# Token lists read ahead of the third expert's weights, kept lists on ScalarE's queue, a short tile's entries on 128 partitions, the eighth expert's weights early

## The chip, the core and the metric

The kernel runs on one NeuronCore of a Trainium2 chip. The metric is device time in microseconds of one execution; the figure for a kernel is the median of several runs. The engines are TensorE (PE), VectorE (DVE), ScalarE (ACT), GpSimd (POOL) and SyncE (SP), which only issues transfers. All transfers run on the core's 16 DMA engines.

## What is computed

One layer of a hybrid decoder: sparse attention with an indexer, a causal pooling branch, a gated merge, a layer norm, a mixture of 64 routed experts (8 per token) with one shared expert, and a second norm with a gated embedding. It works on 512 prompt tokens and 64 sample tokens, 576 rows of width 1024, in float32. The part that matters here:

```python
def moe(h, w_router, router_bias, w_exp13, w_exp2, w_sh13, w_sh2):
    s = jax.nn.sigmoid((h @ w_router).astype(jnp.float32))
    sb = s + router_bias.astype(jnp.float32)
    ...                                     # best 4 of 8 groups, then 8 of 64 experts: eidx
    gate = jnp.take_along_axis(s, eidx, axis=1)
    gate = gate / jnp.sum(gate, axis=-1, keepdims=True) * ROUTED_SCALE
    ...
    y = swiglu(h, w_sh13, w_sh2)            # shared expert
    for e in range(N_EXPERTS):
        y = y + combine[:, e:e + 1] * swiglu(h, w_exp13[e], w_exp2[e])
    return y
```

## The kernel before

The program is written by hand for each engine: every engine has its own list of instructions, runs it strictly in order, and waits on semaphores. PSUM banks go round: a list of jobs made by `plan_banks` gives every product its bank, and the order of each engine must follow that list. The 576 rows are five tiles, four of 128 rows and a last one of 64 (`ROWS`).

The stage of the change lies between the first norm and the expert loop. For every tile TensorE turns the normed rows, computes the router's scores and, later, the shared expert's up product (`shared_up`, job `s13`). VectorE's `route` picks 8 experts per row (mask `selM`), TensorE's `rank` counts with triangular products how many rows before chose the same expert, `pick_gates` puts the gates into `rec`, and `list_goals` turns the rank into a place in a token list and signals `goal_ready`. GpSimd's `enter` then writes the rows' entries (row number, choice number, gate) to the lists in DRAM, one indirect transfer for each of the 8 choices of a tile: forty in all, eight for the tile of 64 rows as well. Each of the 64 experts has one list.

When all entries are in, the lists come back to SBUF as `listed`: for three experts of each four the first 96 entries ("main"), for every fourth expert, whose weights are kept over three passes, 32 entries for each pass ("kept"). SyncE reads them in six transfers (lines 796 and 797). ScalarE repeats the row numbers (`spread`), TensorE turns them (lines 1638 to 1640, job `lists`), VectorE makes row numbers and gates of them (2153 to 2156) and signals `index_ready`; only then GpSimd can gather rows (983).

The expert loop has 48 passes. A pass has 128 rows, 96 of three quarters of a main expert's rows and 32 of the kept expert: the up product (line 1659, 64 matmuls of 32 columns each), the activation, the down product (1672), and an indirect write of the results. GpSimd gathers two passes ahead, in four pieces; VectorE turns the gathered rows (`turn_x`, 2135). The weights of an expert are 3 MB, 2 up and 1 down; there are five slots: three for main experts, two for kept ones (0 and 4). SyncE issues their loads in one fixed order (`load_main`, `load_kept`; up half line 759, down half 762), each behind a wait for the pass that frees the slot: up halves for `up`, down halves for `down`.

Around the change the shared expert's second part runs on TensorE: it turns the gated products (job `s13T`, line 1295, read out by ScalarE at 1047) and multiplies them by `w_sh2` (job `s2`, lines 1631 and 1308), two halves for each tile; VectorE adds them to the rows (2147). In that series stand the turning of the lists, after the second tile, and VectorE's first `turn_x`, after the fourth. The loop's first product waits until all `s2` halves are read. `w_sh13` and `w_sh2` lie in two ring slots at `RING`; slot 4 of the experts lies over both, so expert 7 (the eighth, kept) is loaded when the last `s2` half is done. The order of SyncE there is written out:

```python
            sp.wait_ge(goal_ready, NT)
            filled(sp, ("s13T", NT - 1))
            load_main(2)
            sp.wait_ge(entered, 16 * NT * TOPE)
            ...                                   # six list reads
            filled(sp, ("s2", NT - 1, 1))
            load_kept(1)
```

Of the kernel before, what the change touches and what calls it, by code (L numbers as in the profile page):

```python
# [95 lines left out]
def constants():  # L96
# [22 lines left out]
    rec[:, :, :, 1] = rec[:, :, :, 0] * TOPE + np.arange(TOPE)[None, None, :]  # L119
    put("rec", rec)  # L120
# [31 lines left out]
SMALL_HEADS = 2 * H  # L152


def plan_banks():
# [100 lines left out]
    for t in range(NT):  # L256
        for c in range(2) if t < 4 else (1,):
            add(("s2", t, c), "dve")
        if t == 1:
            add(("lists",), "dve")  # L260
# [3 lines left out]
def build(nc, a, o):  # L264
# [14 lines left out]
    with ctx:  # L279
# [153 lines left out]
        SLOTS = [LG + WSLOT * s for s in range(4)] + [RING]  # L433
        w13 = [at(where, KT * 512).rearrange("p (k n) -> p k n", k=KT) for where in SLOTS]
        w2 = [at(where + 16 * KB, 2 * D).rearrange("p (k n) -> p k n", k=2) for where in SLOTS]

# [5 lines left out]

        def list_row(n):
            return n % 3 * (PASSES // 3) + n // 3
# [13 lines left out]
        yt = [at(where, HALF * D).rearrange("p (j n) -> p j n", j=HALF) for where in (RING, LG + 40 * KB, LG + 56 * KB)]  # L458
        wpin = at(LG, 2 * D).rearrange("p (k n) -> p k n", k=2)
        g2, b2 = at(RING + 24 * KB, D), at(RING + 28 * KB, D)  # L460
# [16 lines left out]
        lists = nc.dram_tensor("token_lists", [NE * LIST, 4], F32, kind="Internal").ap()  # L477

# [87 lines left out]
        listed_in = sem("lists_in")  # L566
# [138 lines left out]
        def _(sp):  # L705
# [81 lines left out]
            sp.wait_ge(goal_ready, NT)  # L787
            filled(sp, ("s13T", NT - 1))
            load_main(2)


            sp.wait_ge(entered, 16 * NT * TOPE)
            by_four = lists.rearrange("(q j n) k -> j q n k", j=4, n=LIST)
            per = PASSES // 3
            for i in range(3):
                sp.dma_start(listed[per * i:per * i + per, 0:CAP, :], by_four[i][:, 0:CAP, :]).then_inc(listed_in, 16)
                sp.dma_start(listed[per * i:per * i + per, CAP:P, :], by_four[3][:, 32 * i:32 * i + 32, :]).then_inc(listed_in, 16)
            extra = further_blocks(sp)
            filled(sp, ("s2", NT - 1, 1))
            load_kept(1)  # L800
# [45 lines left out]
        def _(pool):  # L846
# [198 lines left out]
        def _(act):  # L1045
# [181 lines left out]
            for t in range(1, NT):  # L1227
                shared(t)
# [6 lines left out]
            act.wait_ge(listed_in, 96)  # L1235
            copy(spread, listed[:, :, 0].rearrange("p (g i) -> p g i", g=4).unsqueeze(2).broadcast_to([PASSES, 4, 4, 32])).then_inc(spread_ready, 1)
# [51 lines left out]
        def _(pe):  # L1288
# [329 lines left out]
            for t in range(NT):  # L1618
                pe.wait_ge(sha_ready, t + 1)
                turn4(("s13T", t), [shact[t][0:ROWS[t], P * k:P * k + P] for k in range(2)], ROWS[t])  # L1620
            w = weights(pe, "sh2")
            for t in range(NT):
                read(pe, ("s13T", t))
# [9 lines left out]
                if t == 1:  # L1633
                    pe.wait_ge(listed_in, 96)
                    pe.wait_ge(spread_ready, 1)
                    b = claim(pe, ("lists",))
                    for g in range(4):
                        nc.tensor.transpose(b[:, PASSES * g:PASSES * g + PASSES], spread[:, g, :, :].rearrange("p q i -> p (q i)"), ident[0:PASSES, 0:PASSES])
                    nc.tensor.transpose(b[:, 4 * PASSES:5 * PASSES], listed[:, :, 1], ident[0:PASSES, 0:PASSES])
                    ins = nc.tensor.transpose(b[:, 5 * PASSES:6 * PASSES], listed[:, :, 2], ident[0:PASSES, 0:PASSES])  # L1640
                    fills(ins, ("lists",))


# [126 lines left out]
        def _(dve):  # L1770
# [263 lines left out]
            def route(t):  # L2034
# [19 lines left out]
                link(v.tensor_scalar(selM[0:r, t, :], repl[0:r, :], -1.5e30, None, ALU.is_le))  # L2054
                v.tensor_tensor(ggate[0:r, t, :], sr, selM[0:r, t, :], ALU.mult)
# [5 lines left out]
                dve.sem_inc(routed, 1)  # L2061

            def pick_gates(t):
# [6 lines left out]
                v.tensor_reduce(rec[0:r, t, :, 2], pick[0:r], AX, ALU.add)  # L2070

            def list_goals(t):
# [8 lines left out]
                v.tensor_scalar(goal_u[0:r, t, :], goal8[0:r, :], -1.0, None, ALU.add).then_inc(goal_ready, 1)  # L2081
# [32 lines left out]
            shared(0)  # L2114
            route(NT - 1)
            list_goals(NT - 2)
# [22 lines left out]
            for t in range(NT):  # L2139
                r = ROWS[t]  # L2140
                if t == 4:
                    b = take(dve, ("s2", t, 1))
# [8 lines left out]
                if t == 1:  # L2151
                    b = take(dve, ("lists",))
                    v.tensor_scalar(from_row.rearrange("p e g -> p g e"), b[:, 0:4 * PASSES].rearrange("p (g e) -> p g e", g=4),
                                    4.0, const("quarter"), ALU.mult, ALU.add)
                    v.tensor_copy(to_row, b[:, 4 * PASSES:5 * PASSES])
                    frees(v.tensor_copy(gate, b[:, 5 * PASSES:6 * PASSES]), ("lists",))
                    mine(("lists",))
# [116 lines left out]
```

## Time and profile before

| what | us |
|---|---|
| median of three runs | 1365.29 (1365.12 to 1371.73) |
| the profiled execution, its own time | 1370.32 |
| its span, first to last instruction | 1368.7 |
| first product of the expert loop starts at | 666.33 |
| TensorE busy (share of the span) | 1239.2 (91%) |
| VectorE, ScalarE, GpSimd busy | 645.3, 231.0, 470.7 |

Times in the rows below count from the start of the span. The page's groups name line, engine, operation, tensors and shapes with count, busy time and mean, then the engine's idle time before them and what ended it. The timeline gives start, length, engine, line and operation, with the idle time before in brackets. `arena` is the one large SBUF buffer and `ps` are the PSUM banks, so lines tell the parts apart. A float32 matmul shows as two records, which is why eight products are sixteen.

### The profile page before, as it was taken

Reading aid. Unit: us, or ns where it says so; the run is one execution under the profiler, and the core shown is the slowest. Engines: PE = TensorE matmul, PEld = TensorE weight load, DVE = VectorE, ACT = ScalarE, POOL = GpSimd, SP = SyncE. Lnnn points to the kernel's source line nnn. Section 1 sums busy time; section 2 is a strip of 40 time slices with the busy share of each in tenths; the row PEclk is TensorE's granted clock in tenths of the full one; section 3 lists DMA queues with packets and bytes.
Section 4 is the critical chain, followed back from the end, with each engine's and each line's share of the span. In section 5 each row is a group of like instructions: output and inputs, shape, how many; then the busy total and the mean of one; then the engine's idle time right before and its main releaser. Section 6 shows DMA issues by size and latency. Waiting matters only on the chain. (4 is left out here: it accounts for less than half of the span.)

```text
span 1368.7 us, 20749 instructions
## 1 busy us (share of the span) xinstructions
PE 1239.2 (91%) x7495; PEld 519.1 (38%) x7495; DVE 645.3 (47%) x1110; ACT 231.0 (17%) x496; POOL 470.7 (34%) x586
## 2 busy tenths in 40 slices
PE   5999889999999799998899899898999998988896
PEld 3555443445545534554332222222222222223342
DVE  1336579969972533783332323223232232321894
ACT  1124331022233410010011111011110110111210
POOL 5444516212243000254444344444344343430022
PEclk9999989999999999999899999999999999999998
DMA  8233220122111266032689999999999999997851
GB/s 278 63 123 95 62 77 9 62 77 86 24 24 25 78 231 261 32 144 100 232 319 413 402 407 415 416 390 415 395 414 402 400 410 383 416 384 290 369 154 38
DMA packets 97754, 318.65 MB, mean 233 GB/s; under 512 B 51737, under 2 KB 53533, under 8 KB 80120
## 3 DMA queue, kind: packets, MB, share of 16 engines
q1 hardware_dynamic: 74992, 273.11, 51.8%
q0 software_dynamic: 22672, 44.30, 8.8%
q8 instruction: 60, 0.98, 0.3%
q14 instruction: 30, 0.25, 0.1%
HBM read 298.70 MB, written 31.33 MB: 241 GB/s over the span
## 5 line engine op out<-in xcount | busy, mean ns | idle before, releaser
L1659 PE MATMUL ps<-arena 128*32 128x512 f32 x3072 | 356.9, 618 | 44.7 <-DMA arena<-in_w_exp 42.2
L2135 DVE STREAM_TRANSPOSE arena<-arena 128x1024 f32<-128x1024 f32 x48 | 100.0, 2084 | 260.7 <-DMA arena<-h_rows,arena 260.7
L983 POOL DMA_INDIRECT arena<-h_rows,arena x192 | 193.3, 1007 | 76.5 <-issue 75.6
L1659 PEld LDWEIGHTS ps<-arena 128*32 128x32 f32 x3072 | 97.9, 114 | 267.6 <-issue 215.4
L1672 PE MATMUL ps<-arena 128*32 128x512 f32 x1536 | 173.5, 592 | 0.8 <-DVE arena L2169 0.8
L1319 PE MATMUL ps<-arena 128*128 128x512 f32 (+1 forms) x384 | 166.3, 591 | 4.9 <-DMA arena<-in_w_in 4.8
L1047 ACT ACTIVATE arena<-ps 128x512 f32<-128x512 f32 (+5 forms) x226 | 103.0, 486 | 367.4 <-PE ps L1295 198.9
L990 POOL DMA_INDIRECT y_rows<-arena x48 | 48.8, 1017 | 300.8 <-DVE arena L2169 290.0
L1319 PEld LDWEIGHTS ps<-arena 128*128 128x128 f32 x384 | 72.5, 191 | 91.3 <-issue 90.6
L1672 PEld LDWEIGHTS ps<-arena 128*32 128x32 f32 x1536 | 49.5, 110 | 115.6 <-issue 115.6
L1250 ACT ACTIVATE arena<-ps 128x256 f32<-128x256 f32 x48 | 18.4, 384 | 387.7 <-PE ps L1659 387.7
L1295 PE MATMUL ps<-arena 128*128 128x128 f32 (+1 forms) x375 | 56.6, 308 | 19.2 <-DMA arena<-in_x_prompt 8.8
L1911 DVE MAX8 arena<-arena 64x8 f32<-64x2056 f32 x32 | 73.2, 2289 | 0.5
L1913 DVE MATCH_REPLACE8 arena<-arena 64x2056 f32<-64x2056 f32 x32 | 72.8, 2276 | 0.0
L2169 DVE TENSOR_SCALAR arena<-ps,arena 128x512 f32<-128x512 f32 x48 | 36.0, 749 | 66.1 <-PE ps L1672 66.1
L2178 DVE TENSOR_TENSOR arena<-ps,arena 128x256 f32<-128x256 f32 x48 | 19.4, 403 | 90.4 <-ACT arena L1250 90.4
L1047 ACT ACTIVATE arena<-ps,arena 128x512 f32<-128x512 f32 (+1 forms) x56 | 36.6, 660 | 149.7 <-PE ps L1672 147.3
L1295 PEld LDWEIGHTS ps<-arena 128*128 128x128 f32 (+1 forms) x375 | 48.5, 163 | 31.6 <-issue 14.3
L1765 PE MATMUL ps<-arena 128*128 128x512 f32 x128 | 57.7, 610 | 3.1 <-ACT arena L1047 3.1
L946 POOL TENSOR_TENSOR arena<-arena 128x1 f32<-128x1 f32 x32 | 18.1, 564 | 121.4 <-ACT arena L1157 121.4
L1593 PE MATMUL ps<-arena 128*128 128x512 f32 x128 | 55.6, 594 | 0.6 <-ACT arena L1047 0.6
L687 POOL DMA_DIRECT2D arena<-in_cache_kidx x64 | 34.3, 536 | 58.8 <-issue 50.2
(230 smaller groups left out, 1332.1 us busy)
## 6 DMA issues: line engine op xcount, KB each, us to landing
arena<-in_w_exp SPq DMA_DIRECT2D x64, 2048.0 KB, 20.2
arena<-in_w_exp SPq DMA_DIRECT2D x64, 1024.0 KB, 16.0
arena<-y_rows SPq DMA_DIRECT2D x8, 2048.0 KB, 8.6
arena<-in_w_in SPq DMA_DIRECT2D x6, 2048.0 KB, 7.9
arena<-in_x_prompt SPq DMA_DIRECT2D x8, 512.0 KB, 9.6
arena<-in_cache_v SPq DMA_DIRECT2D x128, 32.0 KB, 1.7
arena<-in_w_out SPq DMA_DIRECT2D x2, 2048.0 KB, 12.1
arena<-in_w_ple_gate SPq DMA_DIRECT2D x2, 2048.0 KB, 17.3
```

The costliest lines, as they stand in the source:

```text
L983: pool.indirect_dma_start(out=xg[s][:, 256 * g:256 * g + 256], out_offset=None, in_=h_quarters, in_offset=bass.IndirectOffsetOnAxis(ap=fro ...
L990: pool.indirect_dma_start(out=y_dram, out_offset=bass.IndirectOffsetOnAxis(ap=to_row[:, list_row(e):list_row(e) + 1], axis=0), in_=ye[e % ...
L1047: return nc.scalar.activation(out, in_, ACT.Copy, scale=scale)
L1295: ins = nc.tensor.transpose(b[0:cols, P * j:P * j + rows], src, ident[0:rows, 0:rows])
L1319: ins = mm(b[0:ROWS[t], 0:width], xT[:, k, span(t)], w[:, k, 0:width], start=(k == 0), stop=(k == KT - 1))
L1593: ins = mm(b[:, :], mT[:, k, span(t)], w[c][:, k, :], start=(k == 0), stop=(k == KT - 1))
L1659: ins = mm(ps[e % 3][q, :], xgT[e % 2][:, kk, q], w13[slots[g]][:, kk, :], start=(kk == 0), stop=(kk == KT - 1))
L1672: ins = mm(ps[3 + 2 * (e % 2) + c][q, :], eactT[e % 2][:, kk, q], w2[slots[g]][:, kk, 512 * c:512 * c + 512], start=(kk == 0), stop=(kk == 1))
L1765: ins = mm(ps[n % 4][0:r, :], h2T[q % 2][:, k, 0:r], wpg_parts[k // 4][:, k % 4, 512 * c:512 * c + 512], start=(k == 0), stop=(k == KT - 1))
L1911: v.max(top8[0:NS, 0, :], scoreS).then_inc(step, 1)
L1913: v.match_replace(scoreS, top8[0:NS, 0, :], scoreS, STRUCK).then_inc(step, 1)
L2135: v.transpose(xgT[e % 2].rearrange("p c (g i) -> p g c i", g=4), xg[e % 3].rearrange("p (g j c) -> p g c j", g=4, c=KT)).then_inc(turned, 1)
```

## The change

It has six parts. (1) `route` signals `routed` as soon as the mask is complete, five operations earlier. (2) VectorE makes the places of tile 3 before it routes tile 4. (3) The tile of 64 rows gets its entries on 128 partitions: choices 0 to 3 on the lower half, 4 to 7 on the upper one; the constants, the gates and the places are laid out so, with two half-size operations in place of one, and four transfers enter them instead of eight, 36 in all. (4) SyncE reads the main lists (three transfers) before it loads expert 2; the wait for `goal_ready` is gone; ScalarE reads the kept lists (three transfers) on its own queue, after the sigmoid of tile 2, under a semaphore of its own. (5) ScalarE's `spread` copy stands before its read-outs of the turned gated products, and the lists are turned after the first tile of `s2` instead of the second. (6) Slot 4 is moved within the ring, up half to `RING + 16 KB`, down half to `RING + 8 KB`: expert 7's down half is loaded right after expert 1, its up half behind expert 2, and the second norm's weights take the room at `RING`.

```diff
+    half = np.arange(TOPE // 2)[None, :]
+    rec[:, NT - 1, :TOPE // 2, 0] = (SEQ + p % NS)[:, None]
+    rec[:, NT - 1, :TOPE // 2, 1] = (SEQ + p % NS)[:, None] * TOPE + half + TOPE // 2 * (p // NS)[:, None]
...
-        SLOTS = [LG + WSLOT * s for s in range(4)] + [RING]
+        SLOTS = [(LG + WSLOT * s, LG + WSLOT * s + 16 * KB) for s in range(4)] + [(RING + 16 * KB, RING + 8 * KB)]
...
-            sp.wait_ge(goal_ready, NT)
+            sp.dma_start(*down_weights(4 + 3, 4)).then_inc(w2_in[4], 16)
+            sp.wait_ge(entered, 16 * LIST_WRITES)
+            for i in range(3):
+                sp.dma_start(listed[LIST_ROWS * i:LIST_ROWS * i + LIST_ROWS, 0:CAP, :], by_four[i][:, 0:CAP, :]).then_inc(listed_in, 16)
+            extra = further_blocks(sp)
             filled(sp, ("s13T", NT - 1))
             load_main(2)
...
+            sp.dma_start(*up_weights(4 + 3, 4)).then_inc(w13_in[4], 16)
             filled(sp, ("s2", NT - 1, 1))
-            load_kept(1)
...
-                r = ROWS[t]
+                r = P
                 pool.wait_ge(goal_ready, t + 1)
-                for j in range(TOPE):
+                for j in range(TOPE if t < 4 else TOPE // 2):
...
-            for t in range(1, NT):
-                shared(t)
+            shared(1)
+            shared(2)
+            act.wait_ge(entered, 16 * LIST_WRITES)
+            for i in range(3):
+                act.dma_start(listed[LIST_ROWS * i:LIST_ROWS * i + LIST_ROWS, CAP:P, :], by_four[3][:, 32 * i:32 * i + 32, :]).then_inc(kept_listed_in, 16)
+            shared(3)
+            shared(4)
+            act.wait_ge(listed_in, 48)
+            act.wait_ge(kept_listed_in, 48)
+            copy(spread, ...).then_inc(spread_ready, 1)
...
             for t in range(NT):
+                if t == LISTS_BEFORE:
+                    turn_lists()
                 read(pe, ("s13T", t))
...
                 link(v.tensor_scalar(selM[0:r, t, :], repl[0:r, :], -1.5e30, None, ALU.is_le))
+                dve.sem_inc(routed, 1)
...
                 link(v.tensor_tensor(place[0:r, t, :], incl[0:r, :], selM[0:r, t, :], ALU.mult))
-                dve.sem_inc(routed, 1)
...
             shared(0)
+            list_goals(NT - 2)
             route(NT - 1)
-            list_goals(NT - 2)
             pick_gates(NT - 1)
```

SyncE before the loop, in the kernel before: the load of `w_sh2`, of expert 1 and 2, then the lists and expert 7. `list_places_ready` is `goal_ready`, `list_entries_written` is `entered`, `banks_filled_for_scalar` the last turned product, `banks_filled_for_vector` the last `s2` half.

```order
L715 DMA arena<-in_w_sh2 128x2x1024 [waits banks_filled_for_vector]
L759 DMA arena<-in_w_exp13 128x4096 [waits banks_read_by_vector]
L762 DMA arena<-in_w_exp2 128x2048
L759 DMA arena<-in_w_exp13 128x4096 [waits banks_filled_for_scalar,list_places_ready]
L762 DMA arena<-in_w_exp2 128x2048
L796 DMA arena<-token_lists 16x384 [waits list_entries_written]
L797 DMA arena<-token_lists 16x128
...
L759 DMA arena<-in_w_exp13 128x4096 [waits banks_filled_for_vector]
L762 DMA arena<-in_w_exp2 128x2048
L801 DMA arena<-in_ln2_g 128x1024
```

The same place in the changed kernel:

```order
L727 DMA arena<-in_w_sh2 128x2x1024 [waits banks_filled_for_vector]
L771 DMA arena<-in_w_exp13 128x4096 [waits banks_read_by_vector]
L774 DMA arena<-in_w_exp2 128x2048
L799 DMA arena<-in_w_exp2 128x2048
L804 DMA arena<-token_lists 16x384 [waits list_entries_written]
...
L771 DMA arena<-in_w_exp13 128x4096 [waits banks_filled_for_scalar]
L774 DMA arena<-in_w_exp2 128x2048
L808 DMA arena<-in_w_exp13 128x4096
L810 DMA arena<-in_ln2_g 128x1024 [waits banks_filled_for_vector]
```

The main lists' reads have moved ahead of expert 2, the two halves of expert 7 ahead of the wait for the last `s2` half.

ScalarE from the shared sigmoids to the loop, before; the 48x512 row is the `spread` copy, the 128x2x128 rows read out the turned products.

```order
L1219 ACTIVATE arena<-ps 128x256 [waits banks_filled_for_vector] x3
L1219 ACTIVATE arena<-ps 64x256 [waits banks_filled_for_vector]
L1047 ACTIVATE arena<-ps 128x2x128 [waits banks_filled_for_scalar] x4
L1047 ACTIVATE arena<-ps 128x2x64 [waits banks_filled_for_scalar]
L1047 ACTIVATE arena<-arena 48x512 [waits lists_in]
```

And in the changed kernel:

```order
L1228 ACTIVATE arena<-ps 128x256 [waits banks_filled_for_vector] x2
L1240 DMA arena<-token_lists 16x128 [waits list_entries_written]
...
L1228 ACTIVATE arena<-ps 128x256 [waits banks_filled_for_vector]
L1228 ACTIVATE arena<-ps 64x256 [waits banks_filled_for_vector]
L1056 ACTIVATE arena<-arena 48x512 [waits kept_lists_in,main_lists_in]
L1056 ACTIVATE arena<-ps 128x2x128 [waits banks_filled_for_scalar] x4
L1056 ACTIVATE arena<-ps 128x2x64 [waits banks_filled_for_scalar]
```

The wait for the entries and the three list reads now stand between the sigmoids, and the copy has moved from behind the five read-outs to before them.

## Rows read from the trace of the kernel before

**Rows 1.** The page, costliest groups: the experts' up products.

```profile
L1659 PE MATMUL ps<-arena 128*32 128x512 f32 x3072 | 356.9, 618 | 44.7 <-DMA arena<-in_w_exp 42.2
```

**Rows 2.** Timeline of TensorE, 608 to 676: start us, us, engine, line, operation.

```profile
608.70 1.20 PE L1574 MATMUL ps<-arena 128*128 128x64 f32 x6 [1.22 <-DVEq L2061]
...
610.12 8.28 PE L1584 MATMUL ps<-arena 128*128 128x512 f32 x16
...
639.32 7.13 PE L1631 MATMUL ps<-arena 128*128 128x512 f32 x16
652.07 0.63 PE L1638 MATMUL ps<-arena 48*128 48x48 f32 x4 [5.61 <-issue]
...
652.84 9.13 PE L1631 MATMUL ps<-arena 128*128 128x512 f32 x16
...
666.33 8.77 PE L1659 MATMUL ps<-arena 128*32 128x512 f32 x64 [2.49 <-DVE arena L2147]
```

**Rows 3.** Timeline of VectorE: mask, routing, places, last gated product, first turn.

```profile
607.06 0.20 DVE L2054 TENSOR_SCALAR arena<-arena 128x64 f32<-128x64 f32 x1
...
611.81 0.22 DVE L2038 TENSOR_TENSOR arena<-arena 64x64 f32<-64x64 f32 x1
...
616.89 0.22 DVE L2077 TENSOR_TENSOR arena<-ps,arena 128x64 f32<-128x64 f32 x1
...
617.67 0.17 DVE L2081 TENSOR_SCALAR arena<-arena 128x8 uint32<-128x8 f32 x1
...
638.52 0.42 DVE L2090 TENSOR_TENSOR arena<-ps,arena 64x256 f32<-64x256 f32 x1
...
662.61 2.03 DVE L2135 STREAM_TRANSPOSE arena<-arena 128x1024 f32<-128x1024 f32 x1
```

**Rows 4.** Timeline of ScalarE: sigmoids of tiles 3 and 4, the repeating copy.

```profile
633.97 0.38 ACT L1219 ACTIVATE arena<-ps 128x256 f32<-128x256 f32 x1 [6.48 <-PE ps L1584]
637.59 0.38 ACT L1219 ACTIVATE arena<-ps 64x256 f32<-64x256 f32 x1 [3.23 <-PE ps L1308]
...
650.86 1.11 ACT L1047 ACTIVATE arena<-arena 48x512 f32<-48x512 f32 x1 [11.15 <-DMA arena<-token_lists]
```

**Rows 5.** Timeline of GpSimd: entries of tiles 3 and 4, first gather's pieces.

```profile
618.12 1.16 POOL L964 DMA_INDIRECT token_lists<-arena  x1 [3.96 <-DVE arena L2081]
...
637.04 0.91 POOL L964 DMA_INDIRECT token_lists<-arena  x1 [0.30 <-issue]
655.14 1.06 POOL L983 DMA_INDIRECT arena<-h_rows,arena  x1 [17.19 <-issue]
...
659.12 1.00 POOL L983 DMA_INDIRECT arena<-h_rows,arena  x1 [0.30 <-issue]
```

**Rows 6.** Timeline of SyncE: first list read, expert 7, a down half.

```profile
640.34 0.43 SPq L796 DMA_DIRECT2D arena<-token_lists  x1
...
663.88 0.37 SPq L759 DMA_DIRECT2D arena<-in_w_exp  x1
...
687.51 0.34 SPq L762 DMA_DIRECT2D arena<-in_w_exp  x1
```

**Rows 7.** Issue to landing: page (median us); then L983 in 650 to 680, `h_rows` in all.

```profile
arena<-token_lists SPq DMA_DIRECT2D x3, 24.0 KB, 8.4
arena<-in_cache_kidx SPq DMA_DIRECT2D x64, 32.0 KB, 1.8
DMA to landing us min/median/max: 2.6/4.6/7.5
DMA to landing us min/median/max: 2.6/10.5/12.8
```

**Rows 8.** Stretches: length, busy us of the engines (count), granted clock, DMA share, GB/s.

```profile
652.00:656.00 4.00, 3.93 (x10) 2.23 (x11) 0.69 (x3) 0.00 (x0) 0.86 (x1) 0.50 0.00 0
...
684.00:688.00 4.00, 4.00 (x41) 1.25 (x34) 1.33 (x3) 0.87 (x2) 0.00 (x0) 1.00 0.02 8
```

**Rows 9.** Timeline of TensorE in the loop: the last pass that waits for weights.

```profile
1215.40 9.38 PE L1659 MATMUL ps<-arena 128*32 128x512 f32 x64 [5.89 <-DMA arena<-in_w_exp]
```

More of the change, by code:

```diff
@@ L256, in plan_banks @@
     for t in range(NT):
+        if t == LISTS_BEFORE:
+            add(("lists",), "dve")
         for c in range(2) if t < 4 else (1,):
             add(("s2", t, c), "dve")
-        if t == 1:
-            add(("lists",), "dve")
     return jobs
@@ L432, in build @@
         WSLOT = 24 * KB
[L433 to L435 removed]
+        SLOTS = [(LG + WSLOT * s, LG + WSLOT * s + 16 * KB) for s in range(4)] + [(RING + 16 * KB, RING + 8 * KB)]
+        w13 = [at(where, KT * 512).rearrange("p (k n) -> p k n", k=KT) for where, _ in SLOTS]
+        w2 = [at(where, 2 * D).rearrange("p (k n) -> p k n", k=2) for _, where in SLOTS]
         def main_slot(n):
@@ L457, in build @@
         HALF = TOPE // 2
-        yt = [at(where, HALF * D).rearrange("p (j n) -> p j n", j=HALF) for where in (RING, LG + 40 * KB, LG + 56 * KB)]
+        yt = [at(where, HALF * D).rearrange("p (j n) -> p j n", j=HALF) for where in (RING + 16 * KB, LG + 40 * KB, LG + 56 * KB)]
         wpin = at(LG, 2 * D).rearrange("p (k n) -> p k n", k=2)
-        g2, b2 = at(RING + 24 * KB, D), at(RING + 28 * KB, D)
+        g2, b2 = at(RING, D), at(RING + 4 * KB, D)
         h2T = [at(PV + (8 + 4 * s) * KB, D).rearrange("p (k n) -> p k n", k=KT) for s in range(2)]
@@ L477, in build @@
         lists = nc.dram_tensor("token_lists", [NE * LIST, 4], F32, kind="Internal").ap()
+        by_four = lists.rearrange("(q j n) k -> j q n k", j=4, n=LIST)
         xp = a["x_prompt"].rearrange("a (t p) n -> p (a t) n", p=P)
@@ L1620, in _, with turn_lists @@
                 turn4(("s13T", t), [shact[t][0:ROWS[t], P * k:P * k + P] for k in range(2)], ROWS[t])
+            def turn_lists():
+                pe.wait_ge(listed_in, 48)
+                pe.wait_ge(kept_listed_in, 48)
+                pe.wait_ge(spread_ready, 1)
+                b = claim(pe, ("lists",))
+                for g in range(4):
+                    nc.tensor.transpose(b[:, PASSES * g:PASSES * g + PASSES], spread[:, g, :, :].rearrange("p q i -> p (q i)"), ident[0:PASSES, 0:PASSES])
+                nc.tensor.transpose(b[:, 4 * PASSES:5 * PASSES], listed[:, :, 1], ident[0:PASSES, 0:PASSES])
+                fills(nc.tensor.transpose(b[:, 5 * PASSES:6 * PASSES], listed[:, :, 2], ident[0:PASSES, 0:PASSES]), ("lists",))
             w = weights(pe, "sh2")
             for t in range(NT):
+                if t == LISTS_BEFORE:
+                    turn_lists()
                 read(pe, ("s13T", t))
@@ L1632, in _ @@
                     fills(ins, key)
[L1633 to L1641, printed above, removed]
             def weights_of(e, loaded):
@@ L2140, in _ @@
                 r = ROWS[t]
+                if t == LISTS_BEFORE:
+                    b = take(dve, ("lists",))
+                    v.tensor_scalar(from_row.rearrange("p e g -> p g e"), b[:, 0:4 * PASSES].rearrange("p (g e) -> p g e", g=4),
+                                    4.0, const("quarter"), ALU.mult, ALU.add)
+                    v.tensor_copy(to_row, b[:, 4 * PASSES:5 * PASSES])
+                    frees(v.tensor_copy(gate, b[:, 5 * PASSES:6 * PASSES]), ("lists",))
+                    mine(("lists",))
+                    dve.sem_inc(index_ready, 1)
                 if t == 4:
@@ L2150, in _ @@
                         frees(ins, key)
[L2151 to L2157, printed above, removed]
-                    dve.sem_inc(index_ready, 1)
                 if t == 3:
```

31 lines of the change are left out of this document (18 added, 13 removed).

## The prediction

> **What bounds the kernel now.** I read the page's groups first and look at the line of the experts' up products: 44.7 us of TensorE's idle time stand before it and 42.2 of them end with the arrival of expert weights [rows 1]. So the expert loop is held by the weight stream. The next question is from when. The last pass that waits starts at 1215.40 after 5.89 us [rows 9], but early in the loop the DMA share is 0.02 between 684 and 688 [rows 8]: nothing is in flight, because the next load waits for the first pass's down product and is issued at 687.51 [rows 6]. A queue that is empty has no memory: from there on transfers follow the passes, so the loop as a whole moves with its first product, at 666.33 [rows 2]. That product is the number to work out.
>
> I read TensorE's timeline before it, then who is late there. TensorE does two tiles of the shared expert's second product (639.32, 7.13 us), waits 5.61 us for the lists until 652.07, and then does two more tiles in 9.13 us, two us more than the same work before the wait [rows 2]; the granted clock is 0.50 in 652 to 656 [rows 8], the lower of its levels, 1.2 of 2.4 GHz, after this idle time. The lists are late by this chain: GpSimd's fortieth entry is issued at 637.04 [rows 5]; SyncE issues the reads at 640.34, right behind expert 2's weights [rows 6]; they need 8.4 us at the median [rows 7]; ScalarE, idle 11.15 us, copies at 650.86 for 1.11 us [rows 4]. GpSimd itself had sat idle 3.96 us before the fourth tile's entries, for VectorE's list places at 617.67 [rows 3, 5].
>
> **The change part by part.** The sum is made on the profiled execution: 1370.32 us, of which 1368.7 is the span and 1.6 lies around it. It is 5.0 above the median 1365.29, so I carry the difference over to the median.
>
> *Earlier signal of the choice.* The mask of tile 3 is complete at 607.06 + 0.20 = 607.26 [rows 3]; TensorE waited 1.22 us, to 608.70, for a signal that came five operations later [rows 2]. It can now start at 608.70 - 1.22 = 607.48. TensorE's following work, one chain to the end of the shared up products, comes 1.2 earlier. If the first of them also kept a higher clock (8.28 us for sixteen products, 7.13 for the sixteen at 639.32 [rows 2]) it is up to 1.2 more; I take none.
>
> *Places of tile 3 before routing tile 4 (VectorE).* The place step runs 616.89 to 617.84, 0.95 us. Put at 611.81, where routing tile 4 begins [rows 3], it ends at 612.8, and routing and all behind it comes 0.95 later; TensorE wants that mask at 617, it is there at 616.4. GpSimd ends tile 2 at 618.12 - 3.96 = 614.16 and goes on at 614.46 instead of 618.12 [rows 5].
>
> *Twelve entries for sixteen (GpSimd).* From 618.12 to 637.04 are fifteen steps, 1.26 us each [rows 5]; wider entries may cost a little more, I take 1.28. The twelfth starts at 614.46 + 11 x 1.28 = 628.5 and is written by about 631, against 640. The last tile's places come at about 622.5 (two more short VectorE operations included), before GpSimd needs them at 624.7.
>
> *List reads first, on two queues.* Issued from 631. What was ahead of them, expert 2's weights, now stands behind; expert 7's down weights, moved to 605, are 1 MB that is long landed. The cost of a list read with nothing in flight is not in the trace: at least 1.8 us, a small read by SyncE, at most the 8.4 seen behind 3 MB [rows 7]. I take 2, since the former's conditions are these. Landed by 634.5. ScalarE's three issues are not in the trace; at least nothing, at most what SyncE's take with the gap between them, 0.43 each and about 0.5 with it [rows 6], which I take: ScalarE is free at 632.5. Tile 3's sigmoid, queued behind the wait and the issues, ran at 633.97 [rows 4] and is due 1.2 earlier, at 632.8. So they hide under the up product of tile 3; without that cover they would cost 1.5.
>
> *The copy ahead of the turned products (ScalarE).* It waited at the end; now tile 4's sigmoid (637.59 [rows 4], 1.2 earlier) ends at 636.8, the lists are there, the copy takes 1.11, and the first turned product is read out at 638.2. Queued behind this wait are the read-outs of all five turned products, and TensorE waits for the first. Tile 4's gated product (638.52 + 0.42 on VectorE [rows 3], 1.2 earlier, to 637.7) is turned by 638.2 too. So the second product begins at 638.3, not 639.32: 1.0 gained of the 1.2.
>
> *List turning after one tile.* From 638.3: one tile 3.57 (half of 7.13), turning 0.77 (652.07 to 652.84), three tiles 10.70: to 653.3. Before, the four tiles ended at 652.84 + 9.13 = 661.97 [rows 2]. Gain 8.6 = 1.0 + 5.6 (the wait) + 2.0 (the clock). The tail from there to the loop, 4.36 us, holds VectorE's turn of the first gathered rows (662.61 [rows 3]) and the last tile's two sums. It stays: loop at 657.7.
>
> *What is late next.* GpSimd's first gather starts about 2.3 us after list turning ends at 642.9 (652.84 to 655.14 [rows 2, 5]), at 645.1; its fourth piece, 3.98 later (659.12 [rows 5]), is issued at 649.1. VectorE wants it at 662.61 - 8.6 = 654.0. In the first passes a piece lands in 2.6 us at least and, beside 4 MB of weights, in 7.5 at most [rows 7]: at 651.7 or 656.6, so 0 or 2.6 lost. Now 5 MB of weights (expert 2, expert 7's up half) start at 638.3; before, 3 MB started at 639.48 and were in by 650, so 5 MB and the gather are in by about 654.5. I take 0.8 lost.
>
> The Trainium skill speaks to this place ("DMA: Bandwidth & Descriptors", Queues, rings and completion order): each DMA engine takes turns between the queues that have work, a packet from each. By it a gather doesn't stand behind all the weights on SyncE's queue, and the loss would by my estimate be near 0, which makes the sum -8.6; the 7.5 beside 2.6 in rows 7 agrees that it is slowed and not stopped.
>
> *Expert 7's weights early, the norm's weights.* They leave SyncE's queue at 663.88 [rows 6], 4 MB before the loop's first reload. The queue ran empty at 684 anyway, so nothing for that: 0. The moved addresses change no operation.
>
> Sum: -8.6 + 0.8 = **-7.8**: 1362.5 on the profiled execution, 1357.5 on the median.
>
> **Rivals.**
> A, the gather held by the early weights: in the loop a gather's median is 10.5 us [rows 7]. 649.1 + 10.5 = 659.6, 5.6 behind 654.0: -3.0, 1362.3. For it: 5 MB are ahead. Against: those end by 654.5. A late list read on the fresh queue (8.4) gives about the same: 640.9 instead of 636.8, 4.1 lost.
> B, the loop gives the start back: its end is set by the bytes, 42.2 us of waits [rows 1], and if the stream were the limit from its first byte an earlier TensorE would only wait longer: 0, 1365.3. Against: the empty stretch at 684.
> C, slower: the thirteen waits of the loop average 42.2/13 = 3.25 and the last is 5.89 [rows 1, 9]. A shifted start changes how gathers, scatters and reloads meet. If the mean wait rose to 4.6, halfway between the two, thirteen times 1.3 are +17, net +9, 1374.5. It decides from 0.6 us more per wait. For it: the runs of before lie 6.6 apart with one program. Against: the bytes per pass are unchanged.
> D, better: no gather wait and the clock kept in the up products: -10, 1355.3.
>
> **How the numbers follow.** Forecast 0.52, A 0.19, B 0.12, C 0.08, D 0.09. Half a per cent, about what a measurement of this kernel can tell from no change, is 6.8 us; below 1358.5 counts as faster. The forecast's own bounds are 0 to 2.6 for the gather, with 0.6 more for a clock that falls in the gap before 638: -8.6 to -5.4, so a part of its chance is "same", as are A and B. Faster 0.50, same 0.40, slower 0.10. The range takes in D, A and B and the few us by which runs differ: 1352 to 1367.
>
> **What would show it.** In the profile after: TensorE's wait before the rank of tile 3 gone; twelve entries without a gap from 614.5; list reads issued near 631 and landing in some 2 us; ScalarE's copy before the turned products, at 637; no long wait before the list turning and full clock behind it; loop at about 658; then the same waits for weights, in sum about 42. It is wrong if the first gathered rows are turned much after 654, if the list reads take 8 us, or if the loop from first to last product is longer than before.

## The result and the profile after

The changed kernel takes 1362.9 us (median, 1352.94 to 1366.89), the kernel before 1370.58 (1362.73 to 1376.4), 13 executions each: 7.7 us less, a ratio of 0.9939 with a 95% interval of 0.992 to 0.9958, which is 5.8 to 11.0 us. The forecast was 7.8 us less. Its 1357.5 stood on the earlier median of 1365.29; the median of before itself came out 5.3 higher this time. The prediction called half a per cent "faster": the ratio lies past that line, its interval on both sides of it.

The profiled execution of after took 1364.19 us, its span is 1362.5. I cut every span at three products: the start of tile 0's shared up product (the sixteen records of that form before tile 3's router scores), the first product of the loop, and the last pass that waits for weights (1215.40 in [rows 9]). The first stretch is the **stage** that the change touches.

| us | starts at | stage | loop to last wait | rest | span |
|---|---|---|---|---|---|
| before, the profile of the prediction | 598.12 | 68.21 | 549.07 | 153.30 | 1368.7 |
| before, profiled again (f1, below) | 597.67 | 66.71 | 549.39 | 149.73 | 1363.5 |
| after | 603.23 | 59.24 | 549.13 | 150.90 | 1362.5 |

So 7.5 us against the second profile of before, 9.0 against the first, come out of the stage and nothing out of the loop. Upstream of the stage, where nothing that matters changed, after's profile is 5 us later; that is run to run (last section).

TensorE of after in the stage, as in [rows 2]: start us, us, engine, line, operation, and the idle time before in brackets.

```profile
612.53 0.88 PE L1589 MATMUL ps<-arena 128*128 128x64 f32 x6
...
613.47 7.09 PE L1599 MATMUL ps<-arena 128*128 128x512 f32 x16
621.22 0.68 PE L1589 MATMUL ps<-arena 128*64 128x64 f32 x8 [0.67 <-DVEq L2071]
...
642.24 3.67 PE L1658 MATMUL ps<-arena 128*128 128x512 f32 x8
645.84 0.44 PE L1642 MATMUL ps<-arena 48*128 48x48 f32 x4
...
646.45 10.57 PE L1658 MATMUL ps<-arena 128*128 128x512 f32 x24
...
662.47 8.77 PE L1675 MATMUL ps<-arena 128*32 128x512 f32 x64 [3.59 <-DVE arena L2180]
```

The 5.61 us before the lists are turned are gone, and the 24 records behind them run at 0.44 us each, as the sixteen ahead of the wait in [rows 2]. Two waits are new or longer: 0.67 before the rank of tile 4, and 3.59 (before: 2.49) in front of the loop.

ScalarE, SyncE, GpSimd and VectorE of after, in that order, as in [rows 3 to 6]:

```profile
636.17 1.34 ACTq L1240 DMA_DIRECT2D arena<-token_lists  x3
637.56 0.38 ACT L1228 ACTIVATE arena<-ps 128x256 f32<-128x256 f32 x1 [7.18 <-PE ps L1599]
640.47 0.38 ACT L1228 ACTIVATE arena<-ps 64x256 f32<-64x256 f32 x1 [2.53 <-PE ps L1323]
640.75 1.12 ACT L1056 ACTIVATE arena<-arena 48x512 f32<-48x512 f32 x1
...
636.17 1.28 SPq L804 DMA_DIRECT2D arena<-token_lists  x3
642.31 0.37 SPq L771 DMA_DIRECT2D arena<-in_w_exp  x1
...
643.19 0.43 SPq L808 DMA_DIRECT2D arena<-in_w_exp  x1
...
634.04 0.97 POOL L973 DMA_INDIRECT token_lists<-arena  x1 [0.30 <-issue]
648.75 1.06 POOL L992 DMA_INDIRECT arena<-h_rows,arena  x1 [13.73 <-issue]
...
652.73 1.00 POOL L992 DMA_INDIRECT arena<-h_rows,arena  x1 [0.30 <-issue]
...
658.78 2.02 DVE L2160 STREAM_TRANSPOSE arena<-arena 128x1024 f32<-128x1024 f32 x1 [1.03 <-DMA arena<-h_rows,arena]
```

The copy (640.75) follows the last sigmoid without a wait, where in [rows 4] it stood idle for 11.15. The view of DMA issues (count, KB each, median us from issue to landing) has the list reads, 8.4 before [rows 7], at

```profile
arena<-token_lists SPq DMA_DIRECT2D x3, 24.0 KB, 1.8
arena<-token_lists ACTq DMA_DIRECT2D x3, 8.0 KB, 1.9
```

and the page's costliest groups have the loop's up products, to be held against [rows 1], at

```profile
L1675 PE MATMUL ps<-arena 128*32 128x512 f32 x3072 | 355.4, 617 | 46.0 <-DMA arena<-in_w_exp 42.4
```

42.4 us of waits for weights in the loop, where [rows 1] had 42.2. That the two agree so closely is chance, for the second profile of before has 38.2; the loop's length, 549.13 against 549.07 and 549.39, is the firmer sign that it moved as a block with its first product.

### The profile page after: what moved, and what is told of

It is laid out like the page before. It is cut to its first block and busy times, and to the rows that moved or that the text cites. A ratio compares the mean times of both kernels' runs of the same rounds, so it can differ in the third digit from the quotient of the medians.

```text
span 1362.5 us, 20748 instructions
## 1 busy us (share of the span) xinstructions
PE 1235.0 (91%) x7495; PEld 518.8 (38%) x7495; DVE 645.1 (47%) x1112; ACT 230.2 (17%) x496; POOL 466.7 (34%) x582
## 5 line engine op out<-in xcount | busy, mean ns | idle before, releaser
L1675 PE MATMUL ps<-arena 128*32 128x512 f32 x3072 | 355.4, 617 | 46.0 <-DMA arena<-in_w_exp 42.4
```

What stands on the lines that cost most here:

```text
L1675: ins = mm(ps[e % 3][q, :], xgT[e % 2][:, kk, q], w13[slots[g]][:, kk, :], start=(kk == 0), stop=(kk == KT - 1))
```

## The experiments

Each was profiled in one execution; f3 and f4 were timed in several others as well. The e runs were on one chip, the f runs on another. The diffs are against after, that of e1 against before.

| run | stage | loop to last wait | rest | time |
|---|---|---|---|---|
| f1 before again | 66.71 | 549.39 | 149.73 | 1365.21 |
| e1 order of reads alone | 60.19 | 549.49 | 149.52 | 1358.98 |
| after | 59.24 | 549.13 | 150.90 | 1364.19 |
| e2 expert 2 ahead | 73.39 | 549.04 | 150.20 | 1376.81 |
| e3 forty entries | 62.65 | 547.53 | 150.80 | 1356.23 |
| e4 places late | 62.69 | 550.13 | 149.91 | 1361.89 |
| e5 kept lists on SyncE | 59.21 | 549.33 | 149.48 | 1352.12 |
| e6 eighth expert late | 58.16 | 550.53 | 150.31 | 1363.45 |
| e7 signal late | 60.45 | 548.87 | 150.31 | 1363.53 |
| e8 copy last | 59.50 | 553.25 | 154.18 | 1364.24 |
| f2 forty entries, copy last | 60.80 | 548.80 | 149.71 | 1358.47 |
| f3 combined | 56.62 | 548.10 | 149.68 | 1357.87 (7 runs) |
| f4 combined, early turn | 55.62 | 547.58 | 152.27 | 1353.17 (6 runs) |

Single times differ by more than most effects, so the verdicts rest on the stage. The stage has its own noise: the two profiles of before differ by 1.5 us there. A smaller difference counts only where an idle time or a clock in the rows accounts for it.

**The kernel before, profiled again (f1).** No edit.

> The kernel before, unchanged in its work, looked at a second time. Theory (part of the fall from 68.21 to 59.24 us between the start of tile 0's shared up product and the loop's first product is chance: the profile of before has its shared up product at 8.28 us where every other trace has 7.08): the product takes 7.1 and the stretch 66.5 to 67.3 us. Rival (the long product belongs to the kernel before): 8.2 and 68.0 to 68.5. Both: the loop up to its last waiting pass at 549 plus or minus 1.

Measured: 66.71. TensorE:

```profile
609.17 7.08 PE L1584 MATMUL ps<-arena 128*128 128x512 f32 x16
...
637.37 7.13 PE L1631 MATMUL ps<-arena 128*128 128x512 f32 x16
650.71 0.63 PE L1638 MATMUL ps<-arena 48*128 48x48 f32 x4 [6.21 <-issue]
...
651.49 8.53 PE L1631 MATMUL ps<-arena 128*128 128x512 f32 x16
```

The theory held: the 8.28 us product of [rows 2] did not come again, and 1.5 of the 9.0 us are not to be put down to the change. The slow clock behind the long wait came again: 8.53 against 7.13 here, 9.13 there. Wait and clock together are 7.61 in both profiles (5.61 + 2.00, 6.21 + 1.40).

**The order of the reads alone (e1).** To the kernel before:

```diff
-            filled(sp, ("s13T", NT - 1))
-            load_main(2)
             sp.wait_ge(entered, 16 * NT * TOPE)
             ...                                   # six list reads
             extra = further_blocks(sp)
+            filled(sp, ("s13T", NT - 1))
+            load_main(2)
```

> The kernel before with one thing changed: its six list reads, all on SyncE, stand ahead of expert 2's weights. I measure the stage from the start of tile 0's shared up product to the loop's first product (68.2 us before, 59.2 after). Theory (the lists were late by the weights ahead of them and by the entries): the reads leave at 640 as before, land in about 2 us each, the wait for the lists and the slow clock behind it go (7 us), but the first gather then sets the start, since the entries still end late: stage 62 to 64. Rival (the shortened entries made the gain, the order of the reads is worth little): 66 to 68.

Measured: 60.19, below both ranges. SyncE's first list read, ScalarE's copy, TensorE's list turning and the products behind it, VectorE's first turn, the loop's first product:

```profile
639.10 0.35 SPq L792 DMA_DIRECT2D arena<-token_lists  x1
...
643.08 1.13 ACT L1045 ACTIVATE arena<-arena 48x512 f32<-48x512 f32 x1 [4.89 <-DMA arena<-token_lists]
...
644.88 0.44 PE L1636 MATMUL ps<-arena 48*128 48x48 f32 x4
...
645.49 7.13 PE L1629 MATMUL ps<-arena 128*128 128x512 f32 x16
...
654.59 2.01 DVE L2133 STREAM_TRANSPOSE arena<-arena 128x1024 f32<-128x1024 f32 x1 [1.24 <-DMA arena<-h_rows,arena]
...
658.29 8.70 PE L1657 MATMUL ps<-arena 128*32 128x512 f32 x64 [3.80 <-DVE arena L2145]
```

With forty entries, late places and the copy in its old place the reads go out at 639.10, about where they did before [rows 6], but land in 1.8 us. The copy is done at 644.21, two tiles of products end at 644.9, and the lists are turned without a wait. As the theory had it, the first gather then sets the start, but it costs only 1.24 us on VectorE. So moving two lines of SyncE's program brings 6.5 of the 7.5 us, and all other parts together bring 0.95.

**Expert 2 ahead of the lists again (e2).**

```diff
-            filled(sp, ("s13T", NT - 1))
-            load_main(2)
             sp.dma_start(*up_weights(4 + 3, 4)).then_inc(w13_in[4], 16)
...
+            filled(sp, ("s13T", NT - 1))
+            load_main(2)
             sp.wait_ge(entered, 16 * LIST_WRITES)
```

> The changed kernel with expert 2's weights issued ahead of the main lists again. Theory: SyncE can issue the weights only when the last gated product is turned, the main lists land some 9 us behind, and because ScalarE's copy now stands before the five read-outs all of the shared expert's second product waits behind it, with a slow clock after it: stage 70 to 73, longer than before's 68.2. Rival that the entries made the gain: 61 to 63. The loop from its first product to the last pass that waits stays at 549 us within 4 if it carries a start over, and shrinks by about the delay if the weight stream alone sets its end.

Measured: 73.39, 5 us worse than before and 0.4 above the theory's range. ScalarE, then TensorE:

```profile
652.98 1.11 ACT L1056 ACTIVATE arena<-arena 48x512 f32<-48x512 f32 x1 [12.92 <-DMA arena<-token_lists]
...
654.46 5.94 PE L1658 MATMUL ps<-arena 128*128 128x512 f32 x8 [12.96 <-issue]
...
675.86 8.77 PE L1675 MATMUL ps<-arena 128*32 128x512 f32 x64 [2.48 <-DVE arena L2180]
```

With the copy first, late lists hold the read-outs of the turned products, TensorE waits for the first of them with nothing left to do, and its clock falls: the granted clock is 0.50 from 650 to 658, the lower level, and the products take 5.94 us for 3.67 in after, at 1.00. The same run decides on the loop. It starts 13.4 us later than in after (675.86 against 662.47) and lasts 549.04 us against 549.13: a late start is carried to the end in full.

**Forty entries (e3) and places late (e4).** e3 takes back part 3: the short tile has 64 rows, eight entries, and whole-tile operations on VectorE. e4 takes back part 2:

```diff
-            list_goals(NT - 2)
             route(NT - 1)
+            list_goals(NT - 2)
```

> The changed kernel with the last tile's entries on 64 partitions, eight transfers, forty in all. Theory: the entries end 4.6 us later; in the changed kernel the lists were in about 1.5 us before ScalarE was free to copy, so 3.1 of them reach the start: stage 62 to 63.5. Rival (the entries are hidden, the order of the reads alone made the gain): 59 to 59.5.

> The changed kernel with the places of tile 3 made after the routing of tile 4 again. Theory: GpSimd's entries of tile 3 begin 3.7 us later, less 1.5 of slack at the lists: stage about 61.4; TensorE's wait of 0.67 us before the rank of tile 4 goes. Rival that the entries are hidden: stage 58.5 to 59.2.

Measured: 62.65, within its theory, and 62.69, 1.3 above its own. In e3 ScalarE and TensorE show:

```profile
631.21 1.34 ACTq L1237 DMA_DIRECT2D arena<-token_lists  x3
632.59 0.65 ACT L1225 ACTIVATE arena<-ps 128x256 f32<-128x256 f32 x2 [11.79 <-issue]
...
634.08 0.44 PE L1307 MATMUL ps<-arena 128*128 128x128 f32 x2 [2.42 <-DVEq L2106]
635.18 0.47 PE L1307 MATMUL ps<-arena 64*128 64x64 f32 x2 [0.66 <-DVEq L2106]
635.64 5.15 PE L1655 MATMUL ps<-arena 128*128 128x512 f32 x8
```

Tile 3's sigmoid could have run at about 627.2, when its product ended; it ran at 632.59, behind ScalarE's wait for the entries and its three issues. TensorE then waits 2.42 and 0.66 for the gated products, and its clock falls, 5.15 for 3.67, with 0.67 granted from 636 to 640. In e4:

```profile
635.20 0.65 ACT L1228 ACTIVATE arena<-ps 128x256 f32<-128x256 f32 x2 [11.15 <-issue]
...
636.68 0.44 PE L1310 MATMUL ps<-arena 128*128 128x128 f32 x2 [1.78 <-DVEq L2117]
...
638.27 6.42 PE L1658 MATMUL ps<-arena 128*128 128x512 f32 x8
```

These are the same two waits, and the products take 6.42, with 0.50 granted from 638 to 642, which is why e4 loses as much as e3 though its entries are less late: the reads go out 36.3 us into the stage there, 37.6 in e3, 32.9 in after. The prediction hid ScalarE's wait under tile 3's up product; that cover is real only if the entries are in by then. The copy's place binds as well: ahead of all read-outs, it gets its lists at 634.16 in e3, so with timely sigmoids the second product (635.64) could hardly have begun earlier. No run separates the two waits. In sum e3's second product starts 3.0 us later than in after, its clock costs 1.5, and 1.1 come back because the gather is no longer late. e4 has no wait before the rank of tile 4, so the 0.67 in after is the price of part 2.

**Kept lists on SyncE (e5).** ScalarE's wait and its three reads go; SyncE issues six.

```diff
-            act.wait_ge(entered, 16 * LIST_WRITES)
-            for i in range(3):
-                act.dma_start(...).then_inc(kept_listed_in, 16)
...
+                sp.dma_start(...).then_inc(kept_listed_in, 16)
```

> The changed kernel with the three kept list reads back on SyncE, interleaved with the main ones, all ahead of expert 2. Theory: six issues take 3 us instead of 1.3 on two engines at once, which uses up the slack of about 1.5 us at ScalarE's copy: stage 59.2 to 59.6 (59.24 in the changed kernel). Rival (the second queue matters because reads on it don't stand behind others): 61 or more.

Measured: 59.21 against 59.24. The second queue is worth nothing here. The Trainium skill says ("DMA: Bandwidth & Descriptors", Issuing engines are not separate DMA queues) that issuing from several engines saves only the time of the issues. The 0.03 us agree: the three issues more that SyncE makes in e5 are over before ScalarE is free to copy.

**The eighth expert late (e6).** Part 6's early loads go back behind the last `s2` half.

> The changed kernel with both halves of expert 7 loaded where the kernel before loads them, after the last half of the shared expert. Theory: 3 MB fewer are in flight beside the first gather, the 1.03 us that VectorE waits for it go, and pass 3 still finds its weights: stage 58.2, loop 549. Rival (the early load is what lets the early passes run): stage 59.2, and a wait for weights in front of pass 3, which there is none of in the changed kernel.

Measured: 58.16, 1.08 less than after. VectorE's first turn no longer waits for the gather:

```profile
657.25 2.03 DVE L2157 STREAM_TRANSPOSE arena<-arena 128x1024 f32<-128x1024 f32 x1
```

No pass before the tenth waits for weights, in e6 as in after. So the early eighth expert costs 1.0 us in the stage. Whether it pays that back later is open: e6's loop is 1.40 us longer than after's (550.53), but f3 and f4, which load it late too, have 548.10 and 547.58.

**Signal late (e7).** `dve.sem_inc(routed, 1)` goes back behind the five operations.

> The changed kernel with the signal that the choice is made at the end of the routing again. Theory: TensorE waits 1.2 us before the rank of tile 3 and then does the next up product at a lower clock (8.3 us instead of 7.1), 2.4 us of which 0.7 were lost again before the rank of tile 4 in the changed kernel: stage 60.5 to 61.5. Rival (the clock there has nothing to do with that wait): the product stays at 7.1 and the stage at 59.5 to 60.5.

Measured: 60.45, 1.21 more. TensorE:

```profile
612.85 0.88 PE L1589 MATMUL ps<-arena 128*128 128x64 f32 x6 [1.21 <-DVEq L2077]
...
613.79 7.08 PE L1599 MATMUL ps<-arena 128*128 128x512 f32 x16
```

The wait is back and the product behind it takes 7.08 all the same, as in e1 and f1: the wait by itself does not bring the lower clock. The one long product, 8.28 in [rows 2], did stand behind this wait, and the ten profiles without it show 7.08 or 7.09; whether part 1 also takes away that chance these runs can't tell.

**The copy last (e8).** Part 5 is taken back, both halves:

```diff
-LISTS_BEFORE = 1
+LISTS_BEFORE = 2
...
-            act.wait_ge(listed_in, 48)
-            act.wait_ge(kept_listed_in, 48)
-            copy(spread, ...)
             for t in range(NT):
                 ...                               # read-out of turned product t
+            act.wait_ge(listed_in, 48)
+            act.wait_ge(kept_listed_in, 48)
+            copy(spread, ...)
```

> The changed kernel with ScalarE's copy behind its five read-outs and the lists turned after two tiles, as before. Theory: the lists are no longer late, so TensorE loses nothing itself, but the row numbers come about 3.3 us later, and with them the first gather, which is already 1 us late at VectorE: the start moves by 2 to 3.3: stage 61 to 62.5. Rival (the place of the turning is hidden by VectorE's other work): 59 to 59.5.

Measured: 59.50, only 0.26 more, which is no difference at this noise; my theory of 61 to 62.5 fell. SyncE's load of expert 2, the fourth piece of the gather, the turn that needs it:

```profile
634.75 0.37 SPq L771 DMA_DIRECT2D arena<-in_w_exp  x1
...
648.60 1.00 POOL L992 DMA_INDIRECT arena<-h_rows,arena  x1 [0.30 <-issue]
...
651.47 2.01 DVE L2160 STREAM_TRANSPOSE arena<-arena 128x1024 f32<-128x1024 f32 x1 [1.29 <-DMA arena<-h_rows,arena]
```

Counted from the start of the stage, the piece is issued 3.4 us later than in after (52.93 against 49.50) but the turn starts only 0.25 later (55.80 against 55.55). Here it is 2.9 us behind the piece's own issue, as in e1 with 3 MB ahead (2.8): the gather's own time. In after, e5 and f2, with 5 MB ahead, it is 6.0, 6.0 and 4.2 behind the piece's issue, and always 16.3 to 16.5 behind the load of expert 2. There the landing follows the weights; issued earlier, a gather only waits longer. The landings say so directly: in after the last weights ahead (expert 7's up half, issued at 643.19) land 15.2 us later, at 658.4, and the turn starts at 658.78; in f2 they land 14.8 after 639.20, at 654.0, and the four pieces, issued 1.3 us apart, at 653.3, 653.8, 654.1 and 654.5.

So parts 5 and 6 depend on each other. With the eighth expert late, e6's turn starts 54.45 us into the stage without a wait; a piece issued at 52.93, as in e8, would by its 2.9 us hold it until 55.8. By that estimate part 5 would be worth some 1.3 us beside a late eighth expert; no run shows it. After the stage e8's loop and rest are the longest of all, 4.1 and 3.3 us over after's: its up products in the loop were busy 362.6 us against 355.4. Whether that belongs to the edit one profile can't tell; the two profiles of before differ by 3.6 us in the rest.

**Forty entries with the copy last (f2).** e3 with e8's order, and all six reads on SyncE.

> The kernel after with forty list writes, the copy of the lists behind ScalarE's read-outs, the lists turned after two tiles, and all six reads on SyncE. Theory (the shorter entries matter only because the changed order puts the copy in front of ScalarE's read-outs; with the copy behind them the later arrival of the lists is covered): the stretch is 59.3 to 60.3 us, no 11 us wait on ScalarE. Rival (the entries are worth their 3 us by themselves): 62 to 63.5.

Measured: 60.80, between the two. ScalarE's longest wait there is 2.19 us, for the lists at its copy, and 1.85 of e3's 62.65 are gone. The 1.3 above e8 are the gather again:

```profile
638.32 0.37 SPq L768 DMA_DIRECT2D arena<-in_w_exp  x1
...
650.43 1.00 POOL L990 DMA_INDIRECT arena<-h_rows,arena  x1 [0.30 <-issue]
...
654.59 2.01 DVE L2147 STREAM_TRANSPOSE arena<-arena 128x1024 f32<-128x1024 f32 x1 [2.58 <-DMA arena<-h_rows,arena]
```

SyncE reads the lists first, so later entries and three more issues put expert 2 at 40.83 us of the stage instead of 39.08, and the turn comes 1.30 later with the piece issued at the same place (52.94). How much of the 1.75 is entries and how much is issues no run separates. Against e3 two things changed on ScalarE, its wait for the entries is gone and its copy stands last; no run separates these either, but e3's rows name the wait.

**Combined (f3).** After with e5 and e6, with GpSimd's block numbers loaded ahead of its wait for the index, and with a shorter wait in front of the loop:

```diff
-            for n in range(NB):
-                read(pe, last_in[n])
+            read(pe, ("s2", NT - 2, 1))
             for e in range(PASSES):
                 up_x(e)
+                if e == 0:
+                    for n in range(NB):
+                        read(pe, last_in[n])
```

> The kernel after with the eighth expert's weights late, all six list reads on SyncE, GpSimd's last block numbers loaded ahead of its wait for the index, and TensorE waiting, before the loop's first up product, only for the read-out of the bank which that product fills, for the other banks after it. Theory (in after the loop's first product waits 3.59 us for the last of the shared outputs' read-outs, of which one product can cover most): the stretch is 56 to 57 us, about 2.5 under after, and the time follows. Rival (the wait only moves to the next pass, whose weights then stand in front as in the loop): stretch 56 to 57 but the loop up to its last waiting pass longer by as much, and the time as after.

**With an early turn (f4).** On top of f3:

```diff
-            read(pe, ("s2", NT - 2, 1))
+            read(pe, ("s2", 2, 0))
...
-                if t == 3:
+                if t == 2:
                     turn_x(0)
```

> The kernel of the run before this one with the first gathered tile turned one shared tile earlier, and the first up product waiting for a bank that is read out sooner. Theory: the stretch is 55 to 56.3 us, about 3.5 under after, if the gather has landed by then. Rival (the gather has not landed one tile earlier, VectorE's turn waits for it, and the shared sums behind the turn are late): 57 to 60.

Measured: 56.62 and 55.62, the theory in both. The loop's first product, in f3 and then in f4:

```profile
649.72 7.07 PE L1670 MATMUL ps<-arena 128*32 128x512 f32 x64 [0.95 <-DVE arena L2157]
```

```profile
649.85 7.07 PE L1670 MATMUL ps<-arena 128*32 128x512 f32 x64
```

The wait of 3.59 falls to 0.95 and to none, and the first product takes 7.07 for 8.77. f3's stage is 1.54 below e6's, and the wait there falls by 1.53, from 2.48 to 0.95: of f3's edits the late eighth expert and the shorter wait account for all of it. The loop isn't longer (548.10, 547.58). Against before on one chip (1367.73), f3 is at 1357.87, ratio 0.9928 (0.9901 to 0.9956), and f4 at 1353.17, ratio 0.989 (0.9856 to 0.9924). Their stages are 10.1 and 11.1 us shorter than before's, their medians 9.9 and 14.6 lower; f4's interval (10.4 to 19.7 us) holds 11.1, so the 14.6 is partly the luck of six runs. f4 is the best kernel here. That it beats after is likely, with 3.6 us less in the stage, but the two intervals still touch (0.992 and 0.9924) and no run times the two side by side.

## Why the prediction was right

The mechanism was right: the lists' wait and the slow clock behind it go, the gather takes a little back, and the loop moves as a block. That the sum is right to 0.1 us at the medians is luck, since the interval of the difference is 5.8 to 11.0 us; the profile on which it was made fell by 9.0 in the stage, 1.5 of which did not come again. Most terms hold one by one. They are put against f1, since the first profile held the long product; times from there to after.

| term | predicted | measured |
|---|---|---|
| second product of the shared expert starts earlier | -1.0 | -0.69 |
| wait for the lists | -5.6 | -6.21 |
| clock behind it | -2.0 | -1.40 |
| turning of the lists, seams | 0 | -0.27 |
| the gather | +0.8 | +1.10 |
| sum | -7.8 | -7.47 |

- *Signal.* 1.2 predicted, 1.21 by e7, and taking no clock gain was right.
- *Places of tile 3.* Here a step failed: "TensorE wants that mask at 617, it is there at 616.4". The mask was right (the rank starts 18.0 us into the stage, 616.1 in that profile), but the 617 carried the product of 8.28 us from [rows 2] as if it belonged to the kernel; it takes 7.09, and TensorE waits 0.67. Against f1 TensorE is 1.26 ahead in front of this wait and 0.72 behind it. The 0.2 that the prediction took off at ScalarE's copy did not come: the second product is 0.69 ahead.
- *Twelve entries.* The reads were to go out at 631, 32.9 us after the start of the stage in that profile; in after they go out at 636.17, 32.9 after it.
- *List reads.* 2 taken, 1.8 and 1.9 measured.
- *ScalarE's issues.* 0.5 each, 1.34 for three; they end 0.7 us after tile 3's product instead of ahead of it, and TensorE does not feel it.
- *Copy.* No wait.
- *Wait and clock.* Their sum, 7.6, is exact; the split between them changes from run to run.
- *Gather.* "5 MB and the gather are in by about 654.5", 16.2 us after the weights' start, came out at 16.5. The prediction doesn't say how it gets there (in proportion to the 10.5 us of 3 MB it would be 17.5), so this is partly luck; and its list turning ends at 642.6 by its own terms, not 642.9, which changes nothing. The added wait in front of the loop is 3.59 - 2.49 = 1.10. By e6 this is the price of part 6, which the prediction put at 0 under its own name.

The Trainium skill's rule that each DMA engine takes turns between its queues ("DMA: Bandwidth & Descriptors", Queues, rings and completion order) would, by the prediction's estimate, have had the gather near its own time, a loss near 0. The measured 1.03 on VectorE, and e8 and f2 against after, speak against that for this gather, and the measurement decides: it landed with the end of the weights. The same section says, of transfers that SyncE and ScalarE issue, that a completion signal is written only after all earlier writes of its engine, across queues. If that held for GpSimd's gather it would look alike; no run here tells the two apart.

*Rivals.* A (the gather held for 10.5 us) would have cost 5.6; it was 1.1. B (the loop gives the start back) falls with e2 in the one direction and with f3 and f4 in the other. C (mean wait 4.6 in the loop): 42.4 us in sum, 42.2 and 38.2 in the two profiles of before. D: the clock in the up product was not to be had, but the gather's wait was, by e6.

What the prediction did not see is which part earns the gain. It costed the parts as one chain, each needed by the next. By e1 the order of SyncE's two jobs does nearly all of it. By e2, e3 and e4 the entries and places of parts 2 and 3 matter mostly because ScalarE now waits early, twice, where before it waited at the end with nothing behind it. In the stage of after part 5 and ScalarE's queue are worth nothing that can be told from noise (0.26 and -0.03), and the early eighth expert costs 1.08.

## What to carry to other kernels

A small read on which a chain depends goes ahead of megabytes on the same queue; here two lines were worth 6.5 us of 7.5, before any engine was made faster. An early wait on an in-order engine is free only while its data are early: name what stands behind it, and what it costs if they come late (3.4 us here with the entries 4.6 late, 14 with the reads behind expert 2). Cut the span at fixed products and compare stretches, and profile the kernel before twice; one profile carried 1.5 us in a stage of 68 that the second did not show.

## What the runs showed of the hardware

The stretch ahead of the stage, which is alike in all these kernels but for a few constants, ends between 592.38 us (e5) and 603.23 (after): 10.9 us, more than the effect. One window in it, of after and then of e5: length, busy us of the engines with counts, granted clock, DMA share, GB/s.

```profile
420.00:480.00 60.00, 49.76 (x461) 34.91 (x462) 23.75 (x85) 23.66 (x38) 9.89 (x14) 0.86 0.18 54
```

```profile
420.00:480.00 60.00, 47.56 (x491) 31.89 (x490) 23.96 (x84) 26.44 (x37) 7.22 (x9) 0.97 0.29 94
```

The granted clock there goes with the start of the stage, but not alone. It is 0.97 in e3, e5 and f3, whose stages start at 592.4 to 593.6; 0.94 in f4, e8 and both profiles of before, 594.2 to 598.1; 0.89 in e7, 602.3; 0.86 in e1, e4 and f2, 597.5 to 598.1, and in after, e2 and e6, 602.5 to 603.2. The only kernel profiled twice had 0.94 both times, so that this clock is part of why one program's runs lie 14 us apart (1352.94 to 1366.89) is likely and not shown; what makes it differ, and the rest of the spread, stay open.

The time of the loop's first product varies too. Behind 2.5 us of idle time it took 8.77 us in four profiles (both of before, e2, e4) and 7.07 or 7.08 in two (e3, e6); behind 3.5 to 5.1 us it took 8.4 to 9.9 in all six (after, e1, e5, e7, e8, f2); behind 0.95 or none 7.07 (f3, f4). The granted clock is 0.66 from 662 to 666 in after and 1.00 from 660 to 664 in e6.

A gather beside 5 MB of weights landed 16.3 to 16.5 us after the weights' issue, whether its own last piece was issued 6.0 us ahead of that (after, e5) or 4.2 (f2).
